# One statistics tile split into six in a hybrid retention, pooling and MLP block on eight cores

## The reference, cut to what matters

```python
h   = rmsnorm(x, ln_mix);  z = h @ w_in          # q | k | v | gate | pool channels | branch gates
ret = retention_chunkwise(rotary(q), rotary(k), v)      # 4 heads, chunks of 128 tokens
mu  = mean(ret);  var = mean((ret - mu)**2)             # group norm per token and head, 256 wide
y_ret  = (silu(g) * (ret - mu) * rsqrt(var + EPS) * gn_gain) @ w_ret_up
y_pool = multiscale_pool(pu, pool_w, pool_scale) @ w_pool_up   # causal means over 2, 4, 8, 16 tokens
        # cnt = minimum(t + 1, w): the first tokens of the sequence divide by fewer
x = x + (sigmoid(gA) * y_ret + sigmoid(gB) * y_pool) @ w_o
x = x + relu(rmsnorm(x, ln_mlp) @ w_up)**2 @ w_down
return rmsnorm(x, ln_final)
```

## Time and profile before

| | |
|---|---|
| median of 2 runs | 2329.14 us (2327.91 to 2330.38) |
| the profiled execution's own time | 2335.59 us |
| its span on the slowest core (core 4) | 2334.0 us |
| spans of the eight cores | 2317.8 to 2334.0 us |
| PE, DVE, ACT, POOL busy | 85%, 38%, 34%, 22% of the span |
| first tile (to about 430 us of the span) | PE busy much less than later; DMA share near 0.9 around one gap |

### The profile page before, as it was taken

The page is one execution under the profiler, slowest core; times in us unless marked ns, Lnnn a source line. Parts: engine busy times, 40 slices in busy tenths (PEclk is TensorE's granted clock), DMA queues, the critical chain, the costliest instruction groups (busy, mean ns, idle before and its releaser), DMA issues.

```text
span 2334.0 us, 30673 instructions; the slowest of 8 cores (2317.8 to 2334.0 us)
## 1 busy us (share of the span) xinstructions
PE 1986.5 (85%) x9760; PEld 920.3 (39%) x9760; DVE 881.1 (38%) x1791; ACT 787.9 (34%) x1331; POOL 502.4 (22%) x519
## 2 busy tenths in 40 slices
PE   3536588498899789998899899998899898998897
PEld 1213233243344344443344344443344344443343
DVE  2335432345222742156322642146323543146311
ACT  2525343243323433053232434054231534144220
POOL 0230111123211322024211322023221322023220
PEclk9778899799999999999999899998999999998998
DMA  8966799732444343442444343442444443442342
GB/s 231 270 193 205 210 287 302 245 127 91 169 154 152 127 167 127 145 180 88 167 148 145 127 169 127 155 168 91 165 147 144 145 149 131 155 155 103 121 149 90
DMA packets 64972, 374.52 MB, mean 160 GB/s; under 512 B 6704, under 2 KB 6704, under 8 KB 32048
## 3 DMA queue, kind: packets, MB, share of 16 engines
q1 hardware_dynamic: 55296, 335.57, 42.7%
q0 software_dynamic: 9520, 37.00, 4.5%
HBM read 322.21 MB, written 50.33 MB: 160 GB/s over the span
## 4 chain that ended last, share of the span: by engine, by line
PE 65%; DMA 11%; DVE 10%; ACT 6%; issue 5%; POOL 1%; DVEq 1%; ACTq 0%; SPq 0%; POOLq 0%
PE ps L303 64%; DMA xs<-wall 9%; DMA xs<-x 2%; ACT junk L412 2%; DVE xs L699 2%; DVE stat L555 1%; ACT scr L569 1%; PE ps L428 1%; DVE stat L312 1%; DVE gated L572 1%; DVE St L535 1%; DVE stat L556 1%; DVEq L151 1%; DVE stat L313 1%; ACT gat L516 1%
## 5 line engine op out<-in xcount | busy, mean ns | idle before, releaser
L303 PE MATMUL ps<-ring,hT 128*128 128x512 bf16 x2048 | 463.1, 385 | 30.0 <-POOL hT L674 13.3
L303 PE MATMUL ps<-gat,ring 128*128 128x512 bf16 x2048 | 461.3, 389 | 28.4 <-ACT gat L434 24.9
L303 PE MATMUL ps<-ring,big 128*128 128x512 bf16 x2048 | 446.8, 380 | 9.8 <-ACT ring L369 4.2
L303 PE MATMUL ps<-hT,ring 128*128 128x512 bf16 x1280 | 313.8, 405 | 69.0 <-ACT scr L569 63.7
L303 PEld LDWEIGHTS ps<-gat,ring 128*128 128x128 bf16 x2048 | 203.8, 100 | 284.1 <-issue 55.0
L303 PEld LDWEIGHTS ps<-ring,hT 128*128 128x128 bf16 x2048 | 201.0, 99 | 275.9 <-issue 52.4
L303 PEld LDWEIGHTS ps<-ring,big 128*128 128x128 bf16 x2048 | 199.7, 98 | 254.0 <-issue 17.5
L716 POOL TENSOR_TENSOR big<-scr 128x512 bf16<-128x512 f32 x128 | 138.1, 1079 | 530.2 <-ACT scr L714 529.3
L714 ACT ACTIVATE scr<-ps 128x512 f32<-128x512 f32 x256 | 150.3, 596 | 263.3 <-PE ps L303 227.6
L303 PEld LDWEIGHTS ps<-hT,ring 128*128 128x128 bf16 x1280 | 127.5, 102 | 243.6 <-issue 122.5
L716 DVE TENSOR_TENSOR big<-scr 128x512 bf16<-128x512 f32 x128 | 97.6, 762 | 312.8 <-ACT scr L714 312.7
(11 more groups left out here) (92 smaller groups left out, 1766.4 us busy)
## 6 DMA issues: line engine op xcount, KB each, us to landing
ring<-wscr SPq DMA_DIRECT2D x224, 1024.0 KB, 4.8
xs<-wall SPq DMA_DIRECT2D x128, 512.0 KB, 9.2
wscr<-ring SPq DMA_DIRECT2D x32, 1024.0 KB, 12.2
xs<-x POOLq DMA_DIRECT2D x8, 2048.0 KB, 10.9
out<-xs POOLq DMA_DIRECT2D x8, 2048.0 KB, 10.5
cst<-cosT POOLq DMA_DIRECT2D x8, 128.0 KB, 10.6
cst<-sinT POOLq DMA_DIRECT2D x8, 128.0 KB, 10.2
cfs<-cf POOLq DMA_DIRECT2D x1, 768.0 KB, 10.9
```

The costliest lines, as they stand in the source:

```text
L303: A("pe", lambda e: e.matmul(out, lhsT=lhsT, rhs=rhs, start=start, stop=stop), [lhsT, rhs], [out])
```

## The change

The tile `stat` is replaced by six tiles of 128x64 float32 (256 bytes per partition each): `st_rms` (RMS norm), `st_gn` (`bst`, `mv`), `st_gn2` (`nmr, gv, gy, gt, gh`), `st_fin` (final norm), `st_fx` (POOL's correction columns) and `st_eps` (the constant). No instruction is added, removed or moved, and no operand's size changes. SBUF use grows from 512 to 1536 bytes per partition, and the tile was the last one allocated, so nothing else moves. Lines from L250 on are five higher in the changed kernel.

```diff
-        stat = sb("stat", [128, 128], F32)
+        st_rms = sb("st_rms", [128, 64], F32)
+        st_gn = sb("st_gn", [128, 64], F32)
+        st_gn2 = sb("st_gn2", [128, 64], F32)
+        st_fin = sb("st_fin", [128, 64], F32)
+        st_fx = sb("st_fx", [128, 64], F32)
+        st_eps = sb("st_eps", [128, 64], F32)
...
-        ssq = stat[:, 0:4]
+        ssq = st_rms[:, 0:4]
...
-        bst = stat[:, 32:56].rearrange("p (h s) -> p h s", h=H)
-        mv = stat[:, 56:64].rearrange("p (h s) -> p h s", h=H)
-        nmr = stat[:, 64:68]
-        epsc = stat[:, 120:121]
+        bst = st_gn[:, 0:24].rearrange("p (h s) -> p h s", h=H)
+        mv = st_gn[:, 24:32].rearrange("p (h s) -> p h s", h=H)
+        nmr = st_gn2[:, 0:4]
+        epsc = st_eps[:, 0:1]
...
-                gv = stat[:, 68:72]
-                gy = stat[:, 72:76]
+                gv = st_gn2[:, 4:8]
+                gy = st_gn2[:, 8:12]
...
-                        fx = stat[:, 96:112]
+                        fx = st_fx[:, 0:16]
...
-            fs = stat[:, 84:88]
-            fv = stat[:, 88:92]
-            fy = stat[:, 92:96]
+            fs = st_fin[:, 0:4]
+            fv = st_fin[:, 4:8]
+            fy = st_fin[:, 8:12]
```

More of the change, by code:

```diff
@@ L281, in build_program @@
         diagk = cbt[:, 640:1152].rearrange("p (h c) -> p h c", h=H)
-        ssq = stat[:, 0:4]
[L283 to L286, removed]
-        bst = stat[:, 32:56].rearrange("p (h s) -> p h s", h=H)
-        mv = stat[:, 56:64].rearrange("p (h s) -> p h s", h=H)
-        nmr = stat[:, 64:68]
-        epsc = stat[:, 120:121]
+        ssq = st_rms[:, 0:4]
+        rv = st_rms[:, 4:8]
+        ry = st_rms[:, 8:12]
+        rt = st_rms[:, 12:16]
+        rh = st_rms[:, 16:20]
+        bst = st_gn[:, 0:24].rearrange("p (h s) -> p h s", h=H)
+        mv = st_gn[:, 24:32].rearrange("p (h s) -> p h s", h=H)
+        nmr = st_gn2[:, 0:4]
+        epsc = st_eps[:, 0:1]
         bank_ctr = [0]
@@ L556, in R3a @@
                     A("dve", lambda e, h=h: e.bn_aggr(out=mv[:, h, :], in_=bst[:, h, :]), [bst[:, h, :]], [mv[:, h, :]])
-                gv = stat[:, 68:72]
-                gy = stat[:, 72:76]
-                gt = stat[:, 76:80]
-                gh = stat[:, 80:84]
+                gv = st_gn2[:, 4:8]
+                gy = st_gn2[:, 8:12]
+                gt = st_gn2[:, 12:16]
+                gh = st_gn2[:, 16:20]
                 A("dve", lambda e: e.tensor_scalar(out=gv, in0=mv[:, :, 1], scalar1=EPS, scalar2=None, op0=ALU.add), [mv], [gv])
@@ L740, in final @@
             xsl = xs[sl]
-            fs = stat[:, 84:88]
-            fv = stat[:, 88:92]
-            fy = stat[:, 92:96]
-            ft = stat[:, 112:116]
-            fh = stat[:, 116:120]
+            fs = st_fin[:, 0:4]
+            fv = st_fin[:, 4:8]
+            fy = st_fin[:, 8:12]
+            ft = st_fin[:, 12:16]
+            fh = st_fin[:, 16:20]
             for tb in range(NTB):
```

## The result

The changed kernel takes 2309.55 us (median of 11 runs). The ratio to the kernel before, run beside it, is 0.9916, with a 95% interval from 0.990 to 0.9932: 0.84% less, 19.6 us of 2329.14 (15.8 to 23.3). In some runs of every kernel the cores of one die ran at a lower granted clock, which lifts medians (that of all ten runs of before to 2383.07 us), so ratios and means here leave those runs out. The mean of the changed kernel's other runs is 2308.0 us. Forecast were 2312.6 us, a gain of 16.5 us, and a range from 2304 to 2323.

What follows compares the result with a forecast made beforehand. Bound: PE for about 1900 us, loading and converting weights in a first tile of about 430 us, stalled there by one wait. 22.3 us gained less 5.8 and 0 gives 16.5: 2329.14 to 2312.6 us, range 2304 to 2323.

Steps and rivals of the forecast that it cites:

- that one wait of the five counts: Tile 0, R3a(1): only DVE's L561 wait on POOL's L608 costs anything; without it L561 starts 22.3 us earlier.
- the term for DVE beside POOL: Tile 0: R3a(1) now runs inside the pooling, as in tile 1, and gives back 5.8 us.
- Its extreme case: Rival, another blocking: DVE loses to POOL at every small instruction, 24 us; gain 0 to 4 us, 2327 us; chance 0.06.
- the sum: Whole kernel: 22.3 - 5.8 - 0 = 16.5 us gained, from 2329.14 to 2312.6 us, 0.7% less.
- the conversions: DVE's conversions of chunk 11, now beside POOL: delay is caught up, taken as 0, bounds 0 and 2 us.
- moves as one piece: From 188 us on, the chain of loads and conversions behind chunk 12's issue shifts whole and meets no fixed date.
- the later tiles: Tiles behind the first hold the same waits and work; a change of more than a few us would show it wrong.
- the 19 us that the prediction named as a sign of being wrong: First tile's end: forecast 16.5 us earlier; a shift under 13 or over 19 us means the prediction is wrong.
- the spans of the cores shrink alike: Sign to look for in the changed kernel: spans of all cores shrink alike.
- Loads that give it back: Rival: longer landings, or DVE's delay reaching chunk 13's loads, cut the gain to 4 to 13 us, 2320 us; chance 0.17.
- No contention loss: Rival: DVE's instructions in tile 0 fall better into POOL's gaps; gain 19 to 22.3 us, 2307 us; chance 0.10.
- Slower by PE's clock: Rival: low clock reaches more matmuls, 226 ns more each; with 160 about 2332 us; chance 0.03.

Runs made afterwards that it cites:

- Experiments 1 and 2: 1 (`fx` only): kernel before with only `fx` in its own tile, ratio 0.9911. 2 (`fx` back): changed kernel with `fx` back beside group norm's values, 0.9999.
- experiment 4: Changed kernel with R3a(1)'s reciprocal square root in the first tile made by one ACT square root and one DVE reciprocal: 2305.97 us, ratio 0.9911.
- experiments 6 to 8: 6: changed kernel, experiment 4's edit in every tile, ratio 0.988. 7: see experiment 7. 8: experiment 7's kernel, that edit on R3a(2) instead, 2277.57 us, 0.9774.
- experiment 7: Changed kernel with the pooling held back until R3a(1) is done, in every tile: 2289.21 and 2291.28 us, ratio 0.9854; repeat 2291.59 us, 0.9834.

## Why the prediction was right or wrong

**Right: that one wait of the five counts, and its size.** Experiments 1 and 2 isolate it, and without POOL's work the gap in SP's loads shrinks by 22.3 us.

**Right: the term for DVE beside POOL.** 5.8 us were taken from tile 1; SP's gap has 6.3 us of it, of which 0.5 is that tile 0's R3a(1) took 12.26 and not 11.74 us. The section cited from the Trainium skill ("SBUF — State Buffer", "Who interferes with whom") counts `tensor_scalar` and casts among the DVE instructions that can use two ports and then contend with GpSimd. The trace agrees in that the four conversions took 4.56 us, between the 2.8 of the earlier trace rows and the bound of 5 plus 1.7; which mode they ran in it doesn't show. Its extreme case did not occur: DVE lost 6.3 + 2.9 us, not 22.

**Wrong: what was set at nothing behind the gap.** This is the step of the sum that failed, in two places with opposite signs. The first is the conversions ("I take 0, bounds 0 and 2 us") with the shift that "moves as one piece". The four conversions took 2.9 us more, and against the issue of chunk 12's loads R3a(2) starts 2.1 us behind where it started 0.8 us ahead of it. It doesn't catch up: ACT's share of the next conversions stands behind it. Issue of each chunk's loads, us behind those of chunk 11, means over the eight cores of one profile each:

| chunk | 12 | 13 | 14 | 15 | 16 |
|---|---|---|---|---|---|
| before | 36.7 | 48.8 | 60.5 | 67.5 | 84.6 |
| changed | 20.7 | 35.7 | 45.3 | 53.9 | 70.5 |
| changed, earlier by | 16.0 | 13.1 | 15.2 | 13.6 | 14.1 |
| without the pooling in tile 0 | 14.4 | 27.6 | 38.3 | 45.1 | 61.9 |

The 13.1 us stand on every core, with `fx` only too. So 2.9 us are lost at chunk 13 and about 2 us are still missing at chunk 16. That R3a(0) to the end of tile 0 is then 16.3 us shorter, against 16.5 forecast, is partly luck: the same stretch takes 289.9 us with `fx` back, and from 271.2 to 276.3 us in four profiles without the wait.

The second is the later tiles ("hold the same waits and the same work"). The changed kernel's profile has tiles 1 to 7 3.5 us shorter. That isn't the splits' work: with all splits but `fx` they take 1889.3 us, as before (1889.2). They are short in the four profiles in which the wait is gone and POOL's work is as before (1885.7, with `fx` only 1886.1 and 1886.0, in experiment 4 1886.9), and long without the pooling in tile 0 (1889.3 and 1889.6) and with the correction free in all tiles (1888.8). So the 3 us seem to come with the missing wait, though no instruction of these tiles differs. How stays open; the profiles only show that the step from one tile's pooling to the next is between 264.0 and 266.8 us on the two cores read in each, with the short ones in changing places.

**The sum.** 16.5 us against 19.6 (15.8 to 23.3) on the slowest core and 16.7, 17.9 and 16.9 on the core mean (the last is 2317.6 - 2300.7, from different batches). The forecast lies inside the interval. Most of the 3.1 us that it is short by is the distance from the mean core to the slowest, for which the sum, worked out on one core, has no term: the time stands 9.8 to 12.8 us above the core mean before, and 7.3 to 10.0 us without the wait. What narrows it stays open. The 4.4 us ahead of the changed place are not the change's: that part takes 122.8 us with `fx` back and 124.3 us with the wait in every tile, so the 129.2 us are one long execution of before. With them the first tile ends 20.7 us earlier, over the 19 us that the prediction named as a sign of being wrong; nor do the spans of the cores shrink alike there (15 to 38 us).

**What was not priced.** The page of before already had in tiles 1 to 7 what experiments 6 to 8 then won: R3a(1) blocked by POOL in each, on PE's path. I had priced that blocking for tile 0 only and left it standing elsewhere as "the same work".

**The rivals.** Loads that give it back: seen in small, and by the road that this rival named, the delay of DVE that reaches chunk 13's loads (2.9 us). No contention loss: refuted by 12.26 us. Slower by PE's clock: the mean granted clock is 0.935 to 0.940 over the cores of before and 0.940 to 0.945 over those of the changed kernel. Its price was also added up wrongly: 160 matmuls at 226 ns are 36.2 us, and on 2312.6 us that is about 2349 us, not 2332.

## What to carry to other kernels

A scheduler that tracks hazards by pieces of a tile makes false waits between engines wherever small values share a piece; look through the chain of waits for a releaser whose output the waiting instruction doesn't read, since one instruction held 22 us of DVE, ACT, SP and PE. When such a wait goes, the freed work lands beside whatever it used to wait for: price it from a place in the same trace where the two already overlap. And a true wait can be worth adding: holding POOL back until the DVE work that PE needs first is done won about as much again as removing the false one (16.8 and 18.0 us of core mean, behind 15.7 and 17.9 us in the same batches).

## What the runs showed of the hardware

DVE's 128x4 instructions of 0.16 us took up to 1.20 us beside POOL's of 1.05 to 1.27 us, POOL's own length unchanged, and about every second instruction of the square root was hit. PE's bubble costs twice: behind a wait of 3.5 us eight matmuls of 512 columns took 3.57 us, 446 ns each, while behind one of 1.26 us eight took 1.89 us:

```profile
145.90 1.89 PE L308 MATMUL ps<-hT,ring 128*128 128x512 bf16 x8 [1.26 <-ACT scr L574]
```

(PE, tile 0, experiment 7). The granted clock is 0.50 in the first stretch, the lower of the clock's two levels (1.2 GHz), and 1.00 in the second, the upper (2.4 GHz).
